# Attention scores of the second block: one-pass products of split q and k in place of fp32 products

## What is computed

```python
# layer 0, stick-breaking attention: 16 heads of 64
z = einsum('bqhd,bkhd->bhqk', q_blk, k) * 64 ** -0.5
earlier = key_pos[None, :] < q_pos[:, None]
log_keep = where(earlier, log_sigmoid(-z), 0.0)
log_after = cumsum(log_keep, axis=3, reverse=True) - log_keep
weight = where(earlier, exp(log_sigmoid(z) + log_after), 0.0)
o = einsum('bhqk,bkhd->bqhd', weight, v)

# layer 1, differential attention: 8 heads, each with two maps of 64 (q1, k1 and q2, k2)
visible = key_chunk[None, :] <= q_chunk[:, None]        # chunks of 64 tokens
a = softmax(where(visible, q1 @ k1.T * scale, -1e30)) - lam * softmax(where(visible, q2 @ k2.T * scale, -1e30))
o = einsum('bhqk,bkhd->bqhd', a, v)
```

## Time and profile before

| | |
|---|---|
| median of three runs | 2171.0 us (2169.86 to 2171.64) |
| the profiled execution, its own time | 2173.59 us |
| its span, first to last instruction | 2171.8 us |
| TensorE busy | 2123.1 us, 98% |
| VectorE busy | 1251.4 us, 58% |
| ScalarE busy | 1038.6 us, 48% |
| GpSimd busy | 225.2 us, 10% |
| mean granted TensorE clock | 0.997 of full speed |

### The profile page before, as it was taken

One profiled execution on the slowest core, in us unless ns is written; L12 is line 12 of the kernel. 1 busy time (PEld: TensorE's weight loads), 2 busy tenths in 40 slices (PEclk: granted clock), 3 DMA queues, 4 the chain that ended last, 5 costly groups with the idle time before them and its releaser, 6 DMA issues.

```text
span 2171.8 us, 35977 instructions
## 1 busy us (share of the span) xinstructions
PE 2123.1 (98%) x15046; PEld 1687.2 (78%) x15046; DVE 1251.4 (58%) x2246; ACT 1038.6 (48%) x2012; POOL 225.2 (10%) x240
## 2 busy tenths in 40 slices
PE   8999999999999999999999999999999999999999
PEld 6777676777787887877777888888777777888887
DVE  6667667666654456655556543444577766443442
ACT  6656565566655235656665332233455554322331
POOL 1112222321120000200001000000110101000000
PEclk9999999999999999999999999999999999999999
DMA  4221221221223432121111323222212112222222
GB/s 179 101 79 64 69 76 50 80 78 51 79 69 129 148 136 97 59 78 48 50 59 63 105 96 110 80 97 100 96 64 64 64 60 97 97 97 97 97 97 78
DMA packets 36227, 186.76 MB, mean 86 GB/s; under 512 B 4560, under 2 KB 4944, under 8 KB 16992
## 3 DMA queue, kind: packets, MB, share of 16 engines
q1 hardware_dynamic: 36064, 184.45, 24.7%
HBM read 172.86 MB, written 7.90 MB: 83 GB/s over the span
## 4 chain that ended last, share of the span: by engine, by line
PE 89%; DVE 6%; ACT 3%; issue 2%; DMA 0%; SPq 0%; POOL 0%; DVEq 0%; ACTq 0%
PE ps L1833 87%; PE ps L1836 1%; ACT arena L2781 1%; DVE spl L2287 1%; ACT spl L2784 1%; ACT hh L2781 0%; DVE x L2646 0%; DMA raw<-wstream 0%; DVE x L2404 0%; DVE arena L2589 0%; DVE x L2575 0%; DVE arena L2487 0%; DVE arena L2571 0%; DVE arena L2306 0%; DVE hl L2597 0%
## 5 line engine op out<-in xcount | busy, mean ns | idle before, releaser
L1833 PE MATMUL ps<-hh,spl 128*128 128x512 f32 (+1 forms) x3152 | 1025.2, 399 | 6.4 <-DVE hl L2579 2.1
L1833 PEld LDWEIGHTS ps<-hh,spl 128*128 128x128 f32 x3152 | 584.8, 189 | 141.2 <-issue 20.5
L1833 PE MATMUL ps<-hl,spl 128*128 128x512 f32 (+1 forms) x1568 | 619.7, 395 | 0.0
L2287 DVE TENSOR_TENSOR spl<-raw,spl 128x512 fp32r<-128x512 f32 x596 | 423.9, 735 | 157.5 <-ACT spl L2784 156.6
L1833 PE MATMUL ps<-arena_r,spl 128*128 128x512 f32 x1968 | 468.4, 392 | 10.5 <-DVE arena_r L2299 8.7
L1833 PEld LDWEIGHTS ps<-arena_r,spl 128*128 128x128 f32 x1968 | 371.7, 189 | 90.3 <-issue 10.8
L2784 ACT ACTIVATE spl<-raw 128x512 fp32r<-128x512 f32 x596 | 345.4, 620 | 142.7 <-PE ps L1833 137.5
L1833 PEld LDWEIGHTS ps<-hl,spl 128*128 128x128 f32 x1568 | 295.7, 189 | 62.9 <-issue 8.4
L1833 PE MATMUL ps<-arena 32*32 32x32 f32 (+6 forms) x5664 | 218.2, 224 | 16.4 <-issue 10.1
L2781 ACT ACTIVATE arena<-arena 128x512 f32<-128x512 f32 (+3 forms) x220 | 142.5, 649 | 189.2 <-DVE arena L2651 140.8
L1833 PEld LDWEIGHTS ps<-arena 32*32 32x32 f32 (+4 forms) x5664 | 126.1, 116 | 97.8 <-issue 79.9
(11 more groups left out here) (257 smaller groups left out, 2123.8 us busy)
## 6 DMA issues: line engine op xcount, KB each, us to landing
raw<-wstream SPq DMA_DIRECT2D x148, 1024.0 KB, 4.9
arena<-spill SPq DMA_DIRECT2D x17, 256.0 KB, 5.4
GS<-g_rows SPq DMA_DIRECT2D x16, 256.0 KB, 3.3
spill<-x SPq DMA_DIRECT2D x14, 256.0 KB, 2.0
arena<-arena SPq DMA_DIRECT2D x18, 128.0 KB, 2.2
x<-xT SPq DMA_DIRECT2D x4, 512.0 KB, 6.4
spill<-arena SPq DMA_DIRECT2D x8, 256.0 KB, 2.0
x<-xT SPq DMA_DIRECT2D x1, 2048.0 KB, 8.4
```

The source lines that it names most:

```text
L1833: return pe.matmul(out, lhsT, rhs, start=start, stop=stop, skip_group_check=True)
L2287: tt(spl[:, p % 2, 1, c], raw[:, p % 2, c], spl[:, p % 2, 0, c].bitcast(F32), ALU.subtract) \
```

## The change

After `st_q`, `st_k` (layer 0) and `br_out` (layer 1) each of q and k is split: ScalarE copies it to an fp32r tile (`qs_hi`), VectorE subtracts that from it and writes the rest over it as fp32r (`qs_lo`). These are 2 x 8 x 2 = 32 pairs of instructions on 128 by 512. The scores wait for the later `qs_lo` of the two and are three fp32r products for each tile of 64 rows (high by high, and the two cross products) where one fp32 product stood; the mask matmuls follow as before. The two tiles alternate. The splits have lanes of their own in the plan, with priority 2, and the planned TensorE cost of the scores goes from 0.86 to 0.65 us for 512 columns. The slots of q and k have four tiles each, so that the arena grows from 41 to 48 tiles and a scratch area of DMA shrinks. Five semaphores of the first block's gates become one, with the same waits in another count.

```diff
 PRIORITY = {...
-            "rope": 5}
+            "rope": 5, "qspl": 2, "kspl": 2}
...
+    def halves_lane(layer, which, m, made, iqk):
+
+        o.behind(made)
+        yield "AC"
+        o.add("qs_hi", layer, which, m, cost=[("AC", AC_B)]).iqk = iqk
+        yield "DV"
+        o.add("qs_lo", layer, which, m, cost=[("DV", DV_B)]).iqk = iqk
+
     def stick_front(m):
 
-        while m not in qk_of:
+        while m not in qk_of or ("qs_lo", 0, "q", m) not in o.at or ("qs_lo", 0, "k", m) not in o.at:
             yield
-        o.behind(o.at["st_q", m], o.at["st_k", m])
+        o.behind(o.at["qs_lo", 0, "q", m], o.at["qs_lo", 0, "k", m])
...
-            st = o.add("st_z", m, kb, cost=[("PE", 0.2 + 0.86 * f)], u=u)
+            st = o.add("st_z", m, kb, cost=[("PE", 0.2 + 0.65 * f)], u=u)
...
             u.home.give(u)
+            o.spawn("qspl", halves_lane(0, "q", m, st, iqk))
...
             u.home.give(u)
+            o.spawn("kspl", halves_lane(0, "k", m, st, iqk))
...
         rope_tmp.give(i, st)
+        o.spawn(which + "spl", halves_lane(1, which, m, st, iqk))
...
-            st = banked("df_s", m, qb, cost=[("PE", 0.15 + 0.86 * f), ("DV", 0.15 + 1.08 * f), ("AC", 0.25 + 0.42 * f),
+            st = banked("df_s", m, qb, cost=[("PE", 0.15 + 0.65 * f), ("DV", 0.15 + 1.08 * f), ("AC", 0.25 + 0.42 * f),
...
-        NA = 41
+        NA = 48
...
                     if kb == 0:
-                        t = at["st_k", m].u
-                        w.wait_ge(drained[t.b], t.n)
-                        t = at["st_q", m].u
-                        w.wait_ge(drained[t.b], t.n)
-                    q_, k_ = qk_of[q.iqk]
-                    for b in range(2):
-                        r = slice(64 * b, 64 * b + 64)
-                        mm(psum[u.b + b][:, 0:n], k_[r, kb * 128:kb * 128 + 128], q_[r, kb * 128:S], True, False)
+                        w.wait_ge(sem("qs_lo"), max(at["qs_lo", 0, c, m].n for c in "qk"))
+                    qh, ql, kh, kl = (part(0, c, q.iqk) for c in "qk" for part in (qk_hi, qk_lo))
+                    for j, (k_, q_) in enumerate(((kh, qh), (kh, ql), (kl, qh))):
+                        for b in range(2):
+                            r = slice(64 * b, 64 * b + 64)
+                            mm(psum[u.b + b][:, 0:n], k_[r, kb * 128:kb * 128 + 128], q_[r, kb * 128:S], j == 0, False)
...
+                    for i, (q_, k_) in enumerate(((qh, kh), (qh, kl), (ql, kh))):
+                        for j in range(2):
+                            r = slice(64 * j, 64 * j + 64)
+                            mm(psum[u.b + j][:, 0:n], q_[r, qb * 128:n], k_[r, 0:n], i == 0, False)
...
+                elif kind == "qs_lo":
+                    layer, which, m = q.key
+                    lo = qk_full(layer, which, q.iqk)
+                    w.wait_ge(sem("qs_hi"), at[("qs_hi",) + q.key].n)
+                    tt(qk_lo(layer, which, q.iqk), lo, qk_hi(layer, which, q.iqk).bitcast(F32), ALU.subtract) \
+                        .then_inc(sem("qs_lo"), 1)
...
+                elif kind == "qs_hi":
+                    layer, which, m = q.key
+                    if layer == 0:
+                        empty(at["st_" + which, m].u)
+                    else:
+                        w.wait_ge(sem("br_out"), at["br_out", which, m].n)
+                    copy(qk_hi(layer, which, q.iqk), qk_full(layer, which, q.iqk)).then_inc(sem("qs_hi"), 1)
...
-    nc = _bacc.Bacc("TRN2", target_bir_lowering=False, num_devices=1, dynamic_dma_scratch_size=8192)
+    nc = _bacc.Bacc("TRN2", target_bir_lowering=False, num_devices=1, dynamic_dma_scratch_size=1024)
```

More of the change, by code:

```diff
@@ L1428, in rope2_lane @@
         rope_tmp.give(i, st)
+        o.spawn(which + "spl", halves_lane(1, which, m, st, iqk))
     def score_lane(m):
-        while ("br_out", "q", m) not in o.at or ("br_out", "k", m) not in o.at:
+        while ("qs_lo", 1, "q", m) not in o.at or ("qs_lo", 1, "k", m) not in o.at:
             yield
@@ L1443, in score_lane @@
             o.now = 0.0
[L1444 removed]
+            o.behind(o.at["qs_lo", 1, "q", m], o.at["qs_lo", 1, "k", m], p_old)
             yield "PE"
[L1446 removed]
+            st = banked("df_s", m, qb, cost=[("PE", 0.15 + 0.65 * f), ("DV", 0.15 + 1.08 * f), ("AC", 0.25 + 0.42 * f),
                                              ("AC", 0.25 + 0.42 * f)], bank=sbp)
@@ L1648, in build, with qk_hi, qk_full, qk_lo @@
         v8, o8 = wide(0, 8), [A(8 + i) for i in range(8)]
-        qk_of = [(A(16), A(17)), (A(18), A(19)), (A(38), A(39))]
+        qk_at = [[(16, 17, 18, 19), (38, 39, 41, 42), (43, 44, 45, 46)], [(16, 17, 18, 19), (23, 24, 41, 42), (43, 44, 45, 46)]]
+        def qk_hi(layer, which, i):
+            return R(qk_at[layer][i][2 * (which == "k")])
+        def qk_full(layer, which, i):
+            return A(qk_at[layer][i][2 * (which == "k") + 1])
+        def qk_lo(layer, which, i):
+            return R(qk_at[layer][i][2 * (which == "k") + 1])
         sp_of, wt_of = ([A(i, 2) for i in ids] for ids in ((20, 22, 24), (26, 28)))
```

35 lines of the change are left out of this document (15 added, 20 removed).

## The result

The changed kernel takes 2187.9 us (median of four runs, 2185.73 to 2192.23) against 2171.3 us for the kernel before (four runs, 2169.86 to 2173.11). The ratio is 1.0073, with a 95% interval of 1.0062 to 1.0085: slower by 16.5 us, and outside the predicted range. The profiled execution took 2186.4 us; its span is 12.7 us longer than that of before, so the traces hold 12.7 of the 16.5 us.

The account below looks back on a forecast made before the run. TensorE, busy for 98% of the span, was taken to bound the kernel. Products -2.8, splits nothing and the scores' wait +0.7 sum to -2.1 us: 2168.9 us against the median of 2171.0, range 2164.5 to 2176.5.

Parts of the forecast that it names:

- What bounds the kernel: Block 2's attention: TensorE bounds both layers; a microsecond off it is worth one, added work on other engines nothing.
- Part 1: Scores of both layers: three one-pass products replace each fp32 one, saving 0.176 us a sweep, 2.8 us off TensorE.
- Part 2: 32 ScalarE copies and 32 VectorE subtractions: costed at nothing, hidden by the next heads' linear products; bounds 0 and 11.2 us.
- Part 3: Each head's first score waits 1.43 us longer; the plan moves it later; 0.7 us added in layer 0, nothing in layer 1.
- the rival in which the end of layer 0 opens: Rewritten plan closes up the last head's blocks, removing the 1.84 us wait and clock fall: 6.3 us saved, 2164.7; chance 0.20.
- The end of layer 0: Last head of layer 0, TensorE's wait for the last `os_lo`: between 0 and 1.4 us later, taken as 0.7.
- Part 4: Single gate semaphore, arena size, unchanged transfers and SyncE and GpSimd queues: costed at nothing.
- VectorE's queue: Slower rival: in layer 1 a `qs_lo` stands ahead of a weight split TensorE needs; 2175.2 us, chance 0.17.
- tiles of 64 rows do run side by side: Denies the slower rival that one-pass score tiles don't run side by side: 26.7 us more, 2198, chance 0.04.
- their loads don't stand free: Concerns the slower rival where each score weight load waits for the product before it: 12 us more, 2183, chance 0.03.
- the distances aren't shorter: Denies the faster rival that one-pass score products take a quarter of the fp32 time: 2163.2 us, chance 0.02.
- a second fall of the clock: Sign of being wrong: only one stretch at clock 0.50 was expected, after the first TensorE wait near 1158 us.

Follow-up runs that it names:

- the first experiment: The changed kernel's written order, with fp32 score products and no split instructions: 2191.4 us against 2172.8 for the kernel before, ratio 1.0088.
- the plan with 0.70: The kernel before with only the scores' planned TensorE cost cut from 0.86 to 0.70 us at 512 columns: 2176.3 us against 2173.4, ratio 1.0013.

## Why the prediction was wrong

**What bounds the kernel.** Read rightly as far as it goes: TensorE sets the pace of both layers. But "work added to the other engines is worth nothing while their queues keep up" left out that each head is one serial chain through TensorE, VectorE and ScalarE, and that TensorE is full only as long as linear products are left to put between. 1.5 us of idle in 217 showed that the cover sufficed, not how much there was to spare. With the order of before it suffices; in every other order tried it does less well.

**Part 1, the products: the mechanism right, the size off.** I said 2.8 us; the starts give 4.3 and the products alone measured 5.1 (3.0 to 7.6). The mis-sized term is that of 128 columns. I put 0.055 us for the first mask's load behind a short stream, and 0.112 us for a distance; a score took 0.67 us, not 0.73. The forecast of 1.03 us for 512 columns was met. Busy time by engine is not the place to see this: TensorE's fell by 1.0 us only. In layer 0 it fell by 1.7 (290.43 to 288.69), in layer 1 it rose by 2.8 (245.97 to 248.75), where the 10.2 us at half clock add 5.1. The rule of "Back-to-back issue gap" in the Trainium skill's page "TensorE: Matmul & The Clock Gate" (131 and 81 ns) would have given another 6 us, an estimate from that page; the 1.03 us disagrees with it.

**Part 2, the splits: nearly met in this order, wrong as a rule.** "I cost them at nothing: what hides them is the linear products of the next heads, which the plan puts between." In the order that the plan wrote they cost some 1 to 3 us, close to nothing. But placed into the order of before they cost 19.8 us, well above the upper bound of 11.2. The bound counted the 16 subtractions of layer 1 at 0.70 us (in the changed kernel they take 0.88 in the mean) in VectorE's queue; the runs show that ScalarE's exponentials and what follows them are delayed too, and in layer 0 also, where I had read 105 us of slack on VectorE and 92 on ScalarE. Slack in a queue's sum is no slack for the instruction that is next: ScalarE stood 30.9 us in front of the copies.

**Part 3, the wait: the failed step.** "The plan must put the score later; it knows the split's cost and does so." It did, and that was the loss, not the cure. I priced the new order at nothing, and it costs 18.6 us by itself, without a split or a one-pass product in it. Two things in it I had in hand. One is the latency of 1.43 us (the rows give 1.41) in front of each head: I compared it once with the 2.06 us of slack at the end of layer 1 and wrote "so nothing is added there". It isn't added once. The plan's waits alone, with no split issued, cost 10.9 us. From 3.6 us late at the first score the heads are 14.4 us late at the last; that this is the latency added again at each of the eight heads (8 x 1.43 = 11.4 us, an estimate) is my reading. The other is the plan's belief that scores are 0.21 us cheaper at 512 columns, "three times what I find". I used this for the rival in which the end of layer 0 opens, to the good; the discount alone costs 10.0 us to the bad. My reading of it: with cheaper scores the planned TensorE clock advances less, so the plan puts more linear blocks between the steps of a head and has fewer left for the last one. The last score of that run, 7.1 us late, and the 13 blocks left behind it in place of 21 fit this, and so do the 20 that 0.70 leaves, at 2.9 us. Why 0.05 us of planned cost moves that score by seven blocks isn't explained.

**The end of layer 0** was wrong in place and too small. I predicted +0.7 us at the wait for the last `os_lo`. That wait is 1.84 us as before, with one fall of the clock behind it as before (1160.4 us, 3.4 us at 0.50). TensorE's idle time grew by 3.5 us elsewhere in the layer. After, in the timeline and in the waits from 905 to 1165 us:

```profile
1159.16 7.15 PE L1856 MATMUL ps<-arena_r,spl 128*128 128x512 f32 x23 [1.84 <-DVE arena_r L2547]
...
PE ps L1856 <- ACT arena L2809: 4.2, 6, 1.4
```

Waits for exponentials rose from 1.5 us in three to 4.2 us in six. The layer's change by itself measured +3.9.

**Part 4** held: the kernel with the products alone has its larger arena, its one semaphore and its smaller scratch area, and is faster than before.

**The rivals.** VectorE's queue had the right sign and named the right layer, but its mechanism, a `qs_lo` ahead of a weight split that TensorE needs, isn't there: no wait of TensorE on `spl` appears among those that grew. The waits that grew are at the tail of the last head and for attention weights. The others fell: tiles of 64 rows do run side by side, their loads don't stand free, the distances aren't shorter, and the end of layer 0 didn't open. The ends of the range, 2164.5 and 2176.5, aren't the times of the rivals that it names, 2164.7 and 2175.2; with 2187.9 measured that changes nothing.

**What was to show it wrong** did. I had named a second fall of the clock, and there are two more in layer 1, at 1692.9 and at 1798.7 us. They are 5.1 of the 13 us that layer 1 lost in that execution. Over all executions the clock makes about 6 of the 16.5 us, an estimate: the mean granted clock is 0.9953 in the four of the changed kernel and 0.9981 in the thirteen of the kernel before that stand beside the first experiment, each read to three places. The sign itself was badly set. The trace of before has a fall at 226 and one at 1553 us besides the one at 1161 that I named, so it should have counted falls inside the two layers only. The one at 1798.7 lies around the wait of 3.55 us; the one at 1692.9 begins at the end of three waits of up to 1.3 us for attention weights (last section).

**Still open.** How the 19.8 us of the splits in the old order divide between their own time and an engine that stands at a copy whose input is late. Both are in that run; the standing is the larger on ScalarE (30.9 us against 10.1 in layer 0), but no run has one without the other, and the version with the splits in the middle of the head, which took the standing away, put a wait of TensorE in its place. The kernel with the waits alone and the one with waits and discount have their last score behind the same block and differ by 7.7 us (in their traces, cut at equal weight splits, by 4.6 in layer 0 and 3.8 in layer 1); why isn't shown. And how much of the 18.6 us a longer search over orders with the same waits would win back; with all of the split work only the one plan was run. The +2.9 us of the plan with 0.70, which adds no dependence, is the only measure here of what a fresh order costs by chance.

## What to carry to other kernels

Where one order is written out for all engines and the bounding engine is busy for 98%, the order is part of the kernel's tuning: run the new order with the old work before the new work is judged, and price a planner's changed cost as an edit of its own. A latency put in front of a chain that repeats is to be counted in every link, and compared with the independent work that is left at the chain's end, not once with one slack. Look at where each queue would stand still, and not at its sum of slack. A saving on the bounding engine (here 4 to 5 us) is small beside 1.4 us of latency in front of each of eight heads.

## What the runs showed of the hardware

**VectorE is held up by GpSimd.** With the subtraction on GpSimd (`qs_lo`, line 3317 there, sixteen of them at 1440 ns) VectorE's own instructions of the softmax took longer. The groups of layer 1, first of that version, then of the version with the same products and the subtraction on VectorE, then of the kernel before (busy us, mean ns, idle before):

```profile
L2806 DVE TENSOR_SCALAR arena<-arena,small 128x128 f32<-128x128 f32 (+3 forms) x32 | 16.3, 511 | 1.1
L2804 DVE TENSOR_TENSOR small<-small 128x2 f32<-128x2 f32 x32 | 13.8, 431 | 1.1
```

```profile
L2813 DVE TENSOR_SCALAR arena<-arena,small 128x128 f32<-128x128 f32 (+3 forms) x32 | 12.4, 387 | 1.1
L2811 DVE TENSOR_TENSOR small<-small 128x2 f32<-128x2 f32 x32 | 7.9, 246 | 1.1
```

```profile
L2760 DVE TENSOR_SCALAR arena<-arena,small 128x128 f32<-128x128 f32 (+3 forms) x32 | 13.4, 418 | 1.1
L2758 DVE TENSOR_TENSOR small<-small 128x2 f32<-128x2 f32 x32 | 8.4, 263 | 1.1
```

An instruction on 128 by 2 elements goes from 246 (263 before) to 431 ns in the mean. Not every VectorE instruction is hit: the one that takes the difference of the two maps keeps its 551 ns. The timeline of the version with splits in the middle of the head shows one such case by itself:

```profile
1608.02 1.28 POOL L3331 TENSOR_TENSOR arena<-arena 128x512 f32<-128x512 f32 x1 [27.45 <-DMA arena<-arena]
1608.04 1.27 DVE L2818 TENSOR_TENSOR small<-small 128x2 f32<-128x2 f32 x1
```

Two elements per partition take 1.27 us, and end 0.01 us behind the GpSimd instruction that began 0.02 us earlier. In this case VectorE wasn't slowed down but shut out. The Trainium skill's page "SBUF — State Buffer", section "Who interferes with whom", says so: a VectorE instruction with two inputs in SBUF contends with a GpSimd one that reads SBUF, and the ports that they share are an exclusive lock. The trace agrees, with 1.27 us. GpSimd at 10% is thus no free engine for a kernel whose chain runs through small VectorE instructions.

**One-pass products on two tiles of 64 rows run side by side.** In the score above, six products of 512 columns take 0.80 us to the start of the masks, the first load included; one after the other, at the 0.227 us of the earlier trace rows, they would need 1.36.

**Waits and the clock.** The granted clock fell to the lower level in stretches of 3.4 or 6.8 us, in a layer in which TensorE is busy for 95% of the time. Each costs up to half its length, as far as TensorE has work in it. One begins at the end of three waits for attention weights, 2.7 us together and none over 1.3. In the 18 us ahead of it TensorE of the changed kernel is busy for 15.3:

```profile
1675.00:1693.00 18.00, 15.29 (x121) 13.67 (x119) 15.78 (x33) 9.89 (x22) 1.78 (x1) 1.00 0.19 62
```

Others lie around a long wait, as in the kernel with the discount alone:

```profile
1793.70:1800.40 6.70, 5.21 (x12) 4.13 (x13) 3.47 (x6) 2.91 (x5) 0.00 (x0) 0.50 0.00 0
```

A wait of 3.55 us ended at 1795.2 in this stretch. So the time that TensorE waits isn't all that a wait costs. Nor is every fall one of the change: in the kernel before there is one at 226, at 1161 and at 1553 us.
